# Four input loads move from SyncE's DMA queue to ScalarE's, and four squares move behind four copies

## The reference

```python
mem_n = rms_norm(mem, mem_norm)
for i in range(DEPTH):
    h = rms_norm(x, norm_pre_mix[i])
    if i % N_MIXERS == 0:
        proj = h @ w_in_a[j]
        mix = gated_deltanet(proj[..., :IN_A - X_WIDTH], conv_w_a[j], ...)
        mem_q = proj[..., IN_A - X_WIDTH:]
    ...
    cross = memory_attention(mem_q, mem_n @ w_mem_kv[i])
```

## Time and profile before

| What | Value |
|---|---|
| Time, median of 3 runs | 2214.86 us (2214.07 to 2215.92) |
| Time of the profiled execution | 2214.86 us |
| Its span in the profile | 2213.1 us |
| PE busy | 2126.4 us, 96% |
| DVE busy | 1088.5 us, 49% |
| ACT busy | 750.9 us, 34% |
| POOL busy | 178.6 us, 8% |
| Data moved by DMA | 182.81 MB, mean 83 GB/s |
| DMA issues of `STG`, 1 MB each | 163, median 4.8 us to landing |

### The profile page before, as it was taken

How to read it: one execution, slowest core, us unless ns; L and a number is a source line. 1 busy time by engine, 2 the same in 40 slices (tenths; PEclk the granted TensorE clock), 3 DMA queues, 4 the chain that set the end, 5 groups by cost and what they waited for, 6 DMA issues and landing times.

```text
span 2213.1 us, 28771 instructions
## 1 busy us (share of the span) xinstructions
PE 2126.4 (96%) x11819; PEld 1753.0 (79%) x11819; DVE 1088.5 (49%) x1381; ACT 750.9 (34%) x1033; POOL 178.6 (8%) x141
## 2 busy tenths in 40 slices
PE   7999999999999989999899999899999999999998
PEld 7877888788888878767788888788787868888886
DVE  4764655454354453353645445545765335454453
ACT  6444433422222232574422222322463243222222
POOL 3000220300000220001300000401001000000001
PEclk9999999999999999999999999999999999999999
DMA  6231000222222212101222222232131212322221
GB/s 238 82 123 40 5 21 3 74 96 95 99 101 92 106 61 92 39 1 58 70 102 95 95 100 92 102 115 95 57 134 61 92 37 78 110 93 101 95 95 57
DMA packets 27025, 182.81 MB, mean 83 GB/s; under 512 B 2992, under 2 KB 3120, under 8 KB 5424
## 3 DMA queue, kind: packets, MB, share of 16 engines
q1 hardware_dynamic: 25776, 177.67, 22.6%
q0 software_dynamic: 432, 2.62, 0.3%
q10 hardware_dynamic: 720, 1.11, 0.1%
HBM read 179.30 MB, written 2.10 MB: 82 GB/s over the span
## 4 chain that ended last, share of the span: by engine, by line
PE 89%; DVE 6%; ACT 3%; DMA 1%; issue 1%; ACTq 0%; DVEq 0%
PE PS L493 88%; ACT Y L1330 1%; DVE Y L2006 1%; DVE WL L2009 1%; ACT WH L1330 1%; DVE Y L2009 1%; DVE HL L2006 0%; DVE SQ L2009 0%; DMA STG<-weights 0%; DMA MX<-mem_t 0%; DVE PS L2006 0%; PE PS L696 0%; DVE HL L2009 0%; DVE DMX L2616 0%; ACT ABUF L1330 0%
## 5 line engine op out<-in xcount | busy, mean ns | idle before, releaser
L493 PE MATMUL PS<-HH,WH 128*128 128x512 f32 (+1 forms) x1608 | 635.5, 395 | 30.7 <-DVE HL L2006 19.5
L493 PE MATMUL PS<-HL,WH 128*128 128x512 f32 (+1 forms) x1608 | 624.9, 389 | 0.0
L493 PE MATMUL PS<-HH,WL 128*128 128x512 f32 (+1 forms) x1608 | 624.3, 388 | 0.0
L2009 DVE TENSOR_TENSOR WL<-STG,WH 128x2048 fp32r<-128x2048 f32 (+1 forms) x163 | 367.7, 2256 | 293.1 <-ACT WH L1330 293.0
L1330 ACT ACTIVATE WH<-STG 128x2048 fp32r<-128x2048 f32 (+2 forms) x171 | 314.9, 1841 | 538.3 <-PE PS L493 536.1
L493 PEld LDWEIGHTS PS<-HH,WH 128*128 128x128 f32 x1608 | 305.6, 190 | 104.3 <-POOL WL L429 19.4
L493 PEld LDWEIGHTS PS<-HH,WL 128*128 128x128 f32 x1608 | 305.5, 190 | 62.3
L493 PEld LDWEIGHTS PS<-HL,WH 128*128 128x128 f32 x1608 | 305.7, 190 | 61.5 <-issue 2.4
L493 PE MATMUL PS<-UPH,WH 128*128 128x512 f32 x832 | 324.2, 390 | 1.4 <-DVE UPL L2006 1.4
L493 PE MATMUL PS<-UPH,WL 128*128 128x512 f32 x832 | 323.7, 389 | 0.0
L493 PE MATMUL PS<-UPL,WH 128*128 128x512 f32 x832 | 323.7, 389 | 0.0
(11 more groups left out here) (286 smaller groups left out, 2019.5 us busy)
## 6 DMA issues: line engine op xcount, KB each, us to landing
STG<-weights SPq DMA_DIRECT2D x163, 1024.0 KB, 4.8
XT<-x_t SPq DMA_DIRECT2D x2, 1024.0 KB, 9.1
out_t<-Y SPq DMA_DIRECT2D x8, 256.0 KB, 2.0
STG<-weights SPq DMA_DIRECT2D x4, 256.0 KB, 5.6
MX<-mem_t ACTq DMA_DIRECT2D x4, 256.0 KB, 7.7
CON<-consts SPq DMA_DIRECT2D x1, 1024.0 KB, 8.9
Y<-recip_counts POOLq DMA_DIRECT2D x1, 1024.0 KB, 5.7
KVM<-mem_t POOLq DMA_DIRECT2D x1, 1024.0 KB, 7.5
```

The lines of the kernel that those rows point to most:

```text
L493: return pe.matmul(o, l, r, start=start, stop=stop, **kw)
L2009: return dve.tensor_tensor(o, a, b, op)
```

## The change

SyncE's straight-line part ends after unit 1; the loop starts one round earlier and loads units 2 and 3 under the same waits as before. The two halves of `XT`, `CON` and the large part of `PAR` are issued by ScalarE, behind its transfers of `MX` and ahead of its first instruction on data. The four squares that stood behind `KR[1]` are done after `split_hi(5)`, with the other four.

```diff
--- before.py
+++ after.py
@@ -381,15 +381,7 @@
                 sp.dma_start(STG[0][:, k:k + 2, :].rearrange("p k n -> p (k n)"),
                              ws[0, :, k * UC:(k + 2) * UC]).then_inc(sems[f"first{k // 2}"], 16)
             sp.dma_start(STG[1][:, :, :].rearrange("p k n -> p (k n)"), ws[1]).then_inc(sems["load1"], 16)
-            sp.wait_ge(sems["lo"], 1)
-            sp.dma_start(STG[0][:, :, :].rearrange("p k n -> p (k n)"), ws[2]).then_inc(sems["load0"], 16)
-            sp.dma_start(XT[:, 0:4, :], xt_in[:, 0:4, :]).then_inc(sems["x_in0"], 16)
-            sp.dma_start(CON[:, :], con_in).then_inc(sems["const_in"], 16)
-            sp.wait_ge(sems["lo"], 2)
-            sp.dma_start(STG[1][:, :, :].rearrange("p k n -> p (k n)"), ws[3]).then_inc(sems["load1"], 16)
-            sp.dma_start(XT[:, 4:8, :], xt_in[:, 4:8, :]).then_inc(sems["x_in1"], 16)
-            sp.dma_start(PAR[:, P:NPAR], par_in[:, P:NPAR]).then_inc(sems["par_in"], 16)
-            with sp.Fori(2, UNITS // 2) as i:
+            with sp.Fori(1, UNITS // 2) as i:
                 for j in range(2):
                     sp.wait_ge(sems["lo"], lin(j - 1, 2, i))
                     sp.dma_start(STG[j][:, :, :].rearrange("p k n -> p (k n)"),
@@ -1703,6 +1695,10 @@
             act.dma_start(PAR[:, 0:P], par_in[:, 0:P]).then_inc(sems["gains_in"], 16)
             for k in range(0, KD, 2):
                 act.dma_start(MX[:, k:k + 2, :], memt_in[:, k:k + 2, :]).then_inc(sems[f"mem_in{k // 2}"], 16)
+            for k in range(0, KD, 4):
+                act.dma_start(XT[:, k:k + 4, :], xt_in[:, k:k + 4, :]).then_inc(sems[f"x_in{k // 4}"], 16)
+            act.dma_start(CON[:, :], con_in).then_inc(sems["const_in"], 16)
+            act.dma_start(PAR[:, P:NPAR], par_in[:, P:NPAR]).then_inc(sems["par_in"], 16)
 
 
             act.wait_ge(sems["eps"], 2)
@@ -1741,13 +1737,11 @@
             memory_tiles(um + 1, V_MEM[0])
             split_hi(um + 4)
             memory_tiles(um + 2, KR[1])
-            for k in range(4):
-                square("A.in", k, XT[:, k, :])
             act.wait_ge(sems["kv_tr"], 1)
             A(KT_MEM[0][:, :, :].rearrange("p f n -> p (f n)"), PS[:, 5, :], ACT.Copy).then_inc(sems["kv_t"], 1)
             memory_tiles(um + 3, V_MEM[1])
             split_hi(um + 5)
-            for k in range(4, KD):
+            for k in range(KD):
                 square("A.in", k, XT[:, k, :])
             act.wait_ge(sems["kv_tr"], 2)
             A(KT_MEM[1][:, :, :].rearrange("p f n -> p (f n)"), PS[:, 6, :], ACT.Copy).then_inc(sems["kv_t"], 1)
```

## The result

The changed kernel took 2229.09 us in the median of 4 runs (2225.30 to 2230.28), the kernel before 2215.39 us beside it (4 runs, 2214.07 to 2217.36): a ratio of 1.0056 [1.0041, 1.0072]; the brackets hold the 95% interval. That is slower, by more than I said; 2229 lies above the range. Two executions of the last set lie far outside, 9269 us of the kernel before and 4306 us of one experiment, and are in no ratio. So the kernel is slower by a few us, and the size of the recorded difference needs a word of its own.

What follows compares the result with a forecast made beforehand. The prediction took the chain of waits, 89% of it TensorE, to bound the kernel. It added 5.3 us at the start and 0.93 us up to the sum of squares to 2214.86, giving 2221.1 us, range 2215.2 to 2222.8.

Steps and rivals of the forecast that it cites:

- The sign: Whole kernel: the change was forecast to make it slower, with chance 0.58 of slower by over 0.2%.
- the 6 us: Whole kernel: forecast slowdown of 6.23 us, from 5.3 at ScalarE's start and 0.93 up to the sum of squares.
- the held sequencer: ScalarE's start: issues wait on a full queue, holding all behind them; unit 1's `WH` comes 5.3 us late.
- part 3: Start: four more issues ahead of ScalarE's first work cost 5.3 us, bounds 0 and 5.9.
- a limit of about 600 to 630 packets in a queue: DMA queues at the start: at this backlog an issue waits until packets start; chance 0.55.
- the fourth rival: Unit 2's load: ScalarE's queue is emptied first, unit lands at 23.9, 3.8 us after needed; chance 0.05.
- the first rival: Start: no queue limit, issues' 1.8 us covered, packets alternate, unit 2 lands at 20.4; 2216.1 us, chance 0.25.
- Part 1: Before unit 4: unit 3's load comes sooner, VectorE's wait for its `WH` goes, gaining 1.44 us.
- Part 2: Before the sum of squares: squares start 3.06 us later, GpSimd ends at 51.93, and TensorE waits for it from 49.56.

Runs made afterwards that it cites:

- the last set: The unchanged pair timed a third time, together with the last experiments: changed kernel 2222.98 us (12 runs) against 2220.52 (34 runs), ratio 1.0020.
- The small-issues kernel: Kernel before with four more issues of 1 KB each on ScalarE ahead of its first work, other loads staying with SyncE: ratio 1.000.
- the kernel with the filling: Changed kernel with matmuls nobody reads in TensorE's waits before unit 2 and before the sum of squares: 2223.56 us, ratio 1.0016 against the kernel before.
- loads alone: Changed kernel with the first four squares put back in their old place, so only the transfers moved: ratio 1.0020 against the kernel before.
- squares alone: Kernel before with all eight squares behind unit 5's `WH`, loads as before: ratio 1.0018.
- The later two sets: Two repeat timings of the unchanged pair: 2225.37 us against 2218.38, ratio 1.0033, and 2222.98 against 2220.52, ratio 1.0020.
- the kernel before with filling: Kernel before with matmuls nobody reads in TensorE's two long waits behind the layers' MLPs, about 785 and 1428 us: ratio 0.9993.

## Why the prediction was wrong

**The sign and the 6 us.** Slower was right. The 6.2 us that I had stand beside 5.8 at unit 6 and ratios of 1.0033 and 1.0020 (+7.3 and +4.4 us of 2215). But that agreement is luck. At unit 1, where the held sequencer was to cost 5.3 us, 0.5 were measured; another 1.7 us at unit 2, for late data, and 3.0 us of clock, neither of which the sum had, filled the place.

**The step that failed: part 3, "a limit of about 600 to 630 packets in a queue".** It stood for 5.3 of the 6.2 us, and up to 980 waiting packets there is none. The queue ScalarE issues to, up to the end of the ninth issue at 6.19 us:

```profile
q10 hardware_dynamic: 316, 0.39, 21.0%
```

1296 packets had been issued and 316 started, so 980 waited, and no issue had been held: the four took 0.47, 0.76, 0.59 and 0.57 us. The fifth issue, ahead of them at 2.65, was long again with 1.04 us, so its length belongs to the first microseconds and not to a full queue. I had read a threshold out of three backlogs that happened to be alike. The small-issues kernel settles it from the other side: four issues more, and unit 1 0.14 us late.

**What stood in its place: the fourth rival, to which I gave 0.05.** ScalarE's queue was served ahead of unit 2's load. The landing, issue at 13.93 (for the earlier trace rows):

```profile
STG<-weights SPq DMA_DIRECT2D x1, 1024.0 KB, 8.6
```

It landed at 22.5 in place of 17.9, and TensorE started unit 2 2.22 us late; the rival had 3.8. It drew the place right but let the other queue hold the engines to its end at 20.5. The packets show two phases: from 14 to 17 us SyncE's queue got nothing at all, and from 17 to 22.6 both had their turn, as the first rival supposed for the whole time:

```profile
q1 hardware_dynamic: 177, 1.32, 55.7%
q10 hardware_dynamic: 191, 1.08, 46.1%
```

The first rival's terms for the issues were right, its landing at 20.4 was 2.1 us early. The section that I weighed there (the Trainium skill, DMA: Bandwidth & Descriptors, "Issuing engines are not separate DMA queues") was right on the issue time, and the small-issues kernel agrees with 1.000; that section says nothing on whose transfer waits.

**A term that no case had: the clock behind a wait.** I priced waits at their length. The longer wait before unit 2 and the new one before the sum brought a stretch of 3.4 us each at the lower level, together 3.0 us, by the kernel with the filling. My profile of before had no such stretch in the first 180 us, though it had them after long waits elsewhere (0.78 and 0.74 in the two windows above). They could have been priced from there, at least in the range.

**Part 1 held.** VectorE doesn't wait before unit 3's `WL`:

```profile
29.38 2.28 DVE L2003 TENSOR_TENSOR WL<-STG,WH 128x2048 fp32r<-128x2048 f32 x1
```

From unit 3's start to unit 4's TensorE needed 6.42 us in place of 8.17, a gain of 1.75 where I had 1.44. Parts 1 and 2 together cost 0.58 us (2.33 - 1.75), where I had 0.93.

**Part 2 held.** The eight squares start 3.01 us after the copy (I had 3.00), the first addition is the long one (2.37 us; I had 2.75), and the step from unit 4 to the sum grew by 2.33 us where I had a wait of 2.37:

```profile
45.71 2.37 POOL L411 TENSOR_TENSOR SQA<-SQ 128x512 f32<-128x512 f32 x1 [22.73 <-ACT SQ L1322]
48.22 6.99 POOL L415 TENSOR_TENSOR SQA<-SQA,SQ 128x512 f32<-128x512 f32 x5
```

**The sum, done again.** At unit 6: loads alone +1.83 (late unit 2 with its stretch, less the gain at unit 4); squares alone +2.95, or 2.30 without the 0.65 that this profile was late at unit 4; both +5.8. Some 1.7 us of it belongs to neither alone. That is the difference of the waits before the sum, 2.16 us with both and 0.45 with the squares alone: with the loads moved TensorE comes to the sum sooner after unit 3, and the additions don't. Each part alone has one profile, so these shares are a reading and not a measurement.

**The rest of the 13.7 us on record** isn't reproduced. The later two sets give +7.3 and +4.4 us. All seven executions of the changed kernel in the first set lie between 2221.33 and 2230.28 us. The 4 runs of before in the first comparison had a mean of 2215.6, where the next 33, 35 and 34 have 2219 to 2220; the changed kernel's were at mean clocks of 0.976 to 0.978, below the 0.980 of its profiled execution. A range built on one profile and three runs had to allow for a spread of 2211.5 to 2227.6 us in one kernel. Why the clock differs from run to run stays open.

## What to carry to other kernels

When transfers are moved ahead in another engine's queue, count the bytes still in front of the next load that somebody waits for, in all queues together: of 2.1 MB moved ahead about 1 MB was left then, and nobody waited; of 3.6 MB 2.4 were left, and TensorE was 2.2 us late. Price a new wait of TensorE with the clock behind it, from stretches that the same profile shows, and count of a stretch only what lies on work. When the mean granted clock of runs differs, compare tens of runs before you explain a difference of half a per cent; time multiplied by clock helps, to 1 or 2 us here, and only between kernels whose waits are filled alike. And profile a start more than once before you divide 6 us among its parts.

## What the runs showed of the hardware that I had not expected

- A queue took 980 waiting packets without holding its issuer. An issue cost 0.34 us when SyncE issued alone at 13.93, and 0.47 to 0.76 us at 3.7 to 6.2 us.
- A load issued on an idle queue at 13.93 got no packet for 3 us while another queue held 2.4 MB (1.30 from 14 to 17 us and 1.08 after, in the rows above). About 1 us of that passes with nothing ahead too: before, the load issued at 13.16 had its first packets between 14.0 and 14.3. Landings took 4.7 us with nothing ahead, 6.4 with about 1 MB, 8.6 with 2.4 MB in the other queue, and 9.1 with 2.1 MB in its own. Why the new queue's turn comes so late stays open.
- TensorE's clock fell after waits of 1.75 to 3.5 us in nine profiles, and in one after 0.45 us of waiting and sixteen one-column matmuls. But it didn't after a wait of 1.87 us before unit 1 in the squares-only kernel (its window from 17 to 24 us has 1.00), nor after 1.74 before unit 4 in the kernel before, where 1.82 at the same place was followed by a fall in the kernel before with filling; nor after this one of 2.71 us in the kernel before, by its timeline and its window:

```profile
1803.91 0.47 PE L493 MATMUL PS<-HH,WH 128*128 128x512 f32 x1 [2.71 <-DVE HL L2009]
```

```profile
1803.00:1815.00 12.00, 11.09 (x49) 9.22 (x50) 5.49 (x9) 3.69 (x8) 0.00 (x0) 1.00 0.00 0
```
